# Transposing the input by products with a diagonal of its inverse norms

## The reference

```
def _rmsnorm(x, g):
    y = xf * lax.rsqrt(jnp.mean(xf * xf, axis=-1, keepdims=True) + RMS_EPS)
    return y * g
h = _rmsnorm(x, g_mix) * (1 + sc1) + sh1
z = h @ w_in
```

## Time and profile before

| what | value |
|---|---|
| median of 3 runs | 2197.09 us |
| time of the profiled execution | 2196.86 us |
| its span, first to last instruction | 2195.1 us |
| VectorE busy | 875.9 us (40%) |
| ScalarE busy | 564.1 us (26%) |
| mean granted clock of TensorE | 0.991 |
| DMA, mean over the span | 289 GB/s |
| products of the transposed x (L877) | 9.6 us busy, 64 of them |

### The profile page before, as it was taken

The page is one execution under the profiler, slowest core; times in us unless marked ns, Lnnn a source line. Parts: engine busy times, 40 slices in busy tenths (PEclk is TensorE's granted clock), DMA queues, the critical chain, the costliest instruction groups (busy, mean ns, idle before and its releaser), DMA issues.

```text
span 2195.1 us, 26368 instructions
## 1 busy us (share of the span) xinstructions
PE 2111.6 (96%) x10319; PEld 1373.5 (63%) x10319; DVE 875.9 (40%) x1246; ACT 564.1 (26%) x998; POOL 4.7 (0%) x8
## 2 busy tenths in 40 slices
PE   8999999999999999999999899999999989998986
PEld 5687888888887776888888545353534444444432
DVE  4672667666676665436333301212020302021114
ACT  4253432222246664113222511010101110011102
POOL 0000000000000000000000000000000000000000
PEclk9999999999999999999999999999999999999999
DMA  9947675887860001533522799999999999999998
GB/s 365 388 156 284 243 249 190 322 309 279 282 239 26 25 1 43 188 134 121 171 87 87 299 393 405 426 427 427 427 427 427 429 426 428 426 428 426 427 422 310
DMA packets 144065, 634.83 MB, mean 289 GB/s; under 512 B 11987, under 2 KB 29545, under 8 KB 112757
## 3 DMA queue, kind: packets, MB, share of 16 engines
q1 hardware_dynamic: 139348, 625.38, 72.7%
q10 hardware_dynamic: 4640, 8.40, 1.0%
HBM read 621.15 MB, written 12.58 MB: 289 GB/s over the span
## 4 chain that ended last, share of the span: by engine, by line
PE 84%; DMA 12%; DVE 2%; ACT 0%; issue 0%; SPq 0%; DVEq 0%
PE bank L801 24%; PE bank L1308 23%; PE bank L803 14%; DMA e_wide<-in_w_e_up 10%; PE bank L1280 5%; PE bank L987 5%; PE bank L861 3%; PE bank L1080 3%; PE bank L1300 1%; PE bank L1068 1%; DMA e_slot<-in_w_e_down 1%; PE bank L1301 1%; PE bank L770 1%; PE bank L1290 1%; PE bank L1192 1%; PE bank L828 0%
## 5 line engine op out<-in xcount | busy, mean ns | idle before, releaser
L1308 PE MATMUL bank<-e_wide,xgT 128*64 128x512 f32 x1456 | 404.5, 606 | 42.7 <-DMA e_wide<-in_w_e_up 26.4
L1489 ACT ACTIVATE w_hi<-stage 128x1024 fp32r<-128x1024 f32 (+1 forms) x168 | 175.4, 1044 | 601.7 <-PE bank L801 339.8
L1915 DVE TENSOR_TENSOR w_lo<-stage,w_hi 128x1024 fp32r<-128x1024 f32 (+1 forms) x168 | 202.4, 1205 | 304.2 <-ACT w_hi L1489 303.6
L1308 PEld LDWEIGHTS bank<-e_wide,xgT 128*64 128x64 f32 x1456 | 131.4, 139 | 284.6 <-issue 283.7
L1308 PE MATMUL bank<-e_slot,xgT 128*64 128x512 f32 x584 | 207.0, 598 | 0.0
L1308 PE MATMUL bank<-e_wide,heT 128*64 128x512 f32 x672 | 167.4, 594 | 0.0
L801 PE MATMUL bank<-hT_hi,w_hi 128*128 128x512 f32 x512 | 159.1, 392 | 0.0
L801 PE MATMUL bank<-hT_lo,w_hi 128*128 128x512 f32 x512 | 157.9, 390 | 0.0
L801 PE MATMUL bank<-hT_hi,w_lo 128*128 128x512 f32 x512 | 157.7, 389 | 0.0
L2486 DVE TENSOR_TENSOR x<-x,bank 128x512 f32<-128x512 f32 x128 | 79.6, 683 | 191.9 <-PE bank L1301 190.3
L1990 DVE SCALAR_TENSOR_TENSOR ada_acc<-ada_tile,siluc,ada_acc 128x1024 f32<-128x1024 f32 x116 | 148.7, 1282 | 7.6 <-DMA ada_tile<-in_w_ada 2.0
(11 more groups left out here) (363 smaller groups left out, 2962.1 us busy)
## 6 DMA issues: line engine op xcount, KB each, us to landing
e_wide<-in_w_e_up SPq DMA_DIRECT2D x49, 2048.0 KB, 17.3
e_wide<-in_w_e_gate SPq DMA_DIRECT2D x42, 2048.0 KB, 14.9
e_wide<-in_w_e_down SPq DMA_DIRECT2D x42, 2048.0 KB, 17.2
ada_tile<-in_w_ada SPq DMA_DIRECT2D x156, 512.0 KB, 5.9
stage<-in_w_in SPq DMA_DIRECT2D x96, 512.0 KB, 6.7
e_slot<-in_w_e_gate SPq DMA_DIRECT2D x43, 1024.0 KB, 15.8
e_slot<-in_w_e_down SPq DMA_DIRECT2D x41, 1024.0 KB, 17.0
e_slot<-in_w_e_up SPq DMA_DIRECT2D x30, 1024.0 KB, 10.5
```

Source lines behind the costliest of these rows:

```text
L1308: last = mm(acc[h][64 * e:64 * e + 64, :], stationary(e), weights(h, e), start=first, stop=end)
L1489: A(w_hi[:, c % NSPLIT, :, 0:width], stage[:, c % NSTAGE, :, 0:width], ACT.Copy).then_inc(hi_ready, 1)
L1915: V.tensor_tensor(w_lo[:, c % NSPLIT, :, 0:width], stage[:, c % NSTAGE, :, 0:width], w_hi[:, c % NSPLIT, :, 0:width].bitcast(F32), ALU.sub ...
```

## The change

The tile of x is no longer multiplied by its inverse norms. VectorE writes a diagonal of 128x128 instead, the identity times the inverse norm of each token, and TensorE multiplies each piece of the raw tile by this diagonal with an ordinary float32 product, which gives the transposed and normalised piece at once. The diagonals of the four tiles have a place of their own (`norm_diag`, behind `junk`). The sharing of the copies changes: VectorE copies all four banks of tiles 0 and 1, and in tiles 2 and 3 ScalarE copies two banks and VectorE two. `columns` moves behind the last tile's copies in VectorE's list. The counts of the waits are adapted.

```
+X_ACT = (0, 0, 2, 2)
+        norm_diag = at("A", 40 * KB, "norm_diag", [P, T, P])
@@ TensorE
-                        if i == 0:
-                            pe.wait_ge(xT_act, t)
+                        if i < X_ACT[t - 1]:
+                            pe.wait_ge(xT_act, sum(X_ACT[:t - 1]) + i + 1)
                         else:
-                            pe.wait_ge(xT_dve, 3 * (t - 1) + i)
+                            pe.wait_ge(xT_dve, 4 * (t - 1) - sum(X_ACT[:t]) + i + 1)
-                        last = nc.tensor.transpose(bank[i][:, kk * P:(kk + 1) * P], x_sb[:, t, k * P:(k + 1) * P], ident[:, :])
+                        last = mm(bank[i][:, kk * P:(kk + 1) * P], x_sb[:, t, k * P:(k + 1) * P], norm_diag[:, t, :], start=True, stop=True)
@@ ScalarE
-                for i in range(1 if t < T - 1 else 2):
+                for i in range(X_ACT[t]):
-                    act.wait_ge(xT_act, T + 1)
-                    act.wait_ge(xT_dve, 3 * T - 1)
+                    act.wait_ge(xT_act, sum(X_ACT))
+                    act.wait_ge(xT_dve, 4 * T - sum(X_ACT))
@@ VectorE
-                for i in range(1 if t < T - 1 else 2, 4):
+                for i in range(X_ACT[t], 4):
-                V.tensor_scalar(x_sb[:, t, :], x_sb[:, t, :], rstd[:, 4 + t:5 + t], None, ALU.mult).then_inc(xn_ready, 1)
+                V.tensor_scalar(norm_diag[:, t, :], ident[:, :], rstd[:, 4 + t:5 + t], None, ALU.mult).then_inc(xn_ready, 1)
                 if t:
                     transposed_x(t - 1)
+            transposed_x(T - 1)
             columns()
-            transposed_x(T - 1)
```

## The result

The changed kernel takes 2204.89 us, the median of 7 runs (2202.63 to 2209.24), against 2197.09 us of the kernel before (7 runs, 2195.82 to 2198.16): a ratio of 1.0038, with a 95% interval of 1.0028 to 1.0048. It is 7.8 us slower, beyond the range of the prediction and clear of the 0.2% that can be told. The profiled execution is the longest of the seven, 2209.24 us with a span of 2207.4; a second set of runs of the same kernel gave 2203.96 us (6 runs, ratio 1.0032, interval 1.0020 to 1.0044). All times here are of fast runs: two runs in the slow state, one of e7 with 9814 us and one of the kernel before with 3596 us, are left out.

A forecast was written before the change was run, and what follows sets the result against it. Bound up to 99.5 us by the later of TensorE's work and the saturated load queue; 3.2 us lost by the queue less 1.5 given back is 1.7, taken as 1.6: 2196.86 + 1.6 = 2198.5 us, range 2196.2 to 2202.3.

The forecast's parts named there:

- Bound and place: Up to 99.5 us the later of TensorE's work and the saturated queue's bytes counts; behind it a shift goes through.
- The diagonal: Start of the prologue: writing 128 columns takes 0.17 us instead of 1.29, so TensorE's first piece starts at 9.1, 1.12 gained.
- Two passes for one: TensorE's prologue: 128 instructions instead of 64, at 0.112 us each after a slow 3.55 us for 16; 6.8 us added.
- upper bound of 10.3: TensorE's prologue: most us the products could add, if the slow stretch lasts for all 32 of the first tile.
- Copies and `columns`: Prologue's end: one copy after the last bank, `columns` adds 0.66 us, zero products hidden; TensorE's stream 6.1 us later.
- The stock of the queue: SyncE's waits up to about 63 us: loads left in the queue cover most of its later issues.
- thin place of 61 to 62: DMA share of 0.88 in that microsecond, taken to say that the queue was nearly drained then.
- L: Time lost by the queue at SyncE's three waits, making the second `ada_tile` land later: 3.2 us, bounds 0 and 6.1.
- The first wait: SyncE's issue of 29.99 becomes 36.1; older loads last to 37.45, first new bytes come at 37.7, 0.3 us lost.
- Rival B: The queue starves at SyncE's wait for the first shift sum and the shift goes through: about 2203 us, chance 0.14.
- The clock: Behind the `ada_tile` wait: the wait of 2.39 us goes, the clock should stay up, 1.5 us come back.
- L - 1.5: Net delay behind the `ada_tile` wait: queue loss less the time the clock gives back, 3.2 - 1.5 = 1.7 us.

The follow-up runs named there:

- e7: The kernel before with only the new shares of the copies and the small copies moved behind the last one: 2197.76 us, ratio 1.0006.
- e13: The kernel before with only the transpositions of tiles 2 and 3 issued twice, 32 passes more: 2198.78 us, ratio 1.0012.
- e3: The kernel before with each of the 64 transpositions issued twice and nothing else: 2203.13 us, ratio 1.0029.
- e1: The changed kernel with `columns` ahead of the last tile's copies again: 2202.83 us, ratio 1.0026.
- e2: The changed kernel with transpositions of the raw tile in place of the products, normalisation left out: 2196.39 us, ratio 0.9998.
- e5: The changed kernel with loads of weight chunks 4 to 7 and two tables moved ahead of the first wait that empties the queue: 2204.98 us, ratio 1.0037.
- e4: The changed kernel with loads of weight chunks 10 and 11 moved ahead of the load waiting for the first shift sum: 2201.44 us, ratio 1.0019.
- e10: The changed kernel unaltered, run and profiled a second time: 2203.96 us, ratio 1.0032.
- e6: The changed kernel with products by zeros ahead of the awaited `ada_tile` units, adding nothing to bank 7: 2204.14 us, ratio 1.0034.

## Why the prediction was wrong

*Bound and place: right.* Two clocks run up to about 100 us, TensorE's stream and the bytes of one queue, and behind them a shift goes to the end.

*The diagonal: nearly right.* It took 0.29 us, not 0.17. The first piece came at 9.62, not 9.1; 0.37 of that is the first tile of x, whose squares began at 6.71 instead of 6.34 in this execution.

*Two passes for one: right in kind, 1.6 us short in size.* There are 128 records, as forecast. But 32 of them take 3.77 us in the chain, 0.118 each and not 0.112, which is 0.7 us. A product thus adds 0.236 us where a transposition adds 0.119, a factor of 2.0. The Trainium skill ("TensorE: Matmul & The Clock Gate", Terms) gives the transpose mode as 4 times faster for FP32; the runs differ from it, and they decide. And the slow stretch did not keep its 3.55 us: the third bank of tile 0 was full at 15.1, 24 passes in 5.5 us, so some 8 to 9 more passes were slow, about 0.9 us. The last bank was full at 30.39 instead of 28.3. In all the passes added 8.4 us. The upper bound of 10.3 was added up wrongly: the 16 further slow passes are in the 6.8 already, at 0.112 each, so they add 16 x (0.222 - 0.112) = 1.8, and the bound is 8.6. The measured 8.4 lies just under it.

*Copies and `columns`: right.* One copy after the last bank, 0.6 us of small copies, the zero products hidden under the low weights. Shift 8.2 instead of 6.1, all of it from the terms above.

*The stock of the queue: the step that failed.* That "the thin place of 61 to 62 says that the queue was nearly drained then" gave 2.9 us of cover to an issue at 56.91 (61.4 - 56.91 - 1.6) and L = 3.2. Measured L is 8.85. Of the 5.65 us between them 2.1 are the larger shift, 2.9 the cover that was not there, and 0.6 arose between the late issue (8.26) and the landing. In e7, e13, e3 and the change the landing is 1.0, 0.9, 1.0 and 1.1 times the shift, and with SyncE's old order of loads no run has more than 0.8 us of its shift covered (e1; e2 0.6). The thin place was misread. It lies in SyncE's next pause, of 60.04 to 63.64, when the loads issued from 56.91 on are already under way (the first of them lands at 62.1):

```profile
58.87 1.17 SPq L508 DMA_DIRECT2D sh_tile<-in_w_ada  x2
63.64 0.93 SPq L492 DMA_DIRECT2D ada_tile<-in_w_ada  x2
```

So it doesn't tell how long the older loads lasted; the times to landing do (5.2 and 5.5 us before, 3.6 and 5.3 behind an empty queue). Why the share dips at 61 to 62 was not tested.

The first wait was mis-sized in the same way. The prediction let the queue last until its last load landed, 37.45, and lost 0.3 us there; in the change that load lands at 37.7, 10.5 us after its issue, but the engines had little left to move from 35 us on:

```profile
35.00:36.00 1.00, 0.60 (x3) 0.47 (x3) 1.00 (x2) 0.00 (x0) 0.00 (x0) 1.00 0.28 99
36.00:37.00 1.00, 1.00 (x6) 0.77 (x6) 0.16 (x1) 0.00 (x0) 0.00 (x0) 1.00 0.11 40
37.00:38.00 1.00, 1.00 (x11) 0.47 (x13) 0.00 (x0) 0.00 (x0) 0.00 (x0) 1.00 0.01 4
```

That error alone does no harm: e5 shows that an earlier hole only moves, and the prediction's own sum says so too, since its 0.3 + 0.3 + 2.6 is 64.6 - 61.4, in which the first two waits no longer stand. Rival B had the right place and the right mechanism with a chance of 0.14, and its bound of 6.1 for L was only the too small shift.

*The clock: not given back.* TensorE did wait, 3.1 us in all, and the low clock came back and lasted longer. Where it did stay up, the prediction's sum L - 1.5 fits the start of the first dense block to 0.1 us: it is 6.7 us later in e3 (8.2 - 1.5), 1.9 in e13 (3.4 - 1.5), 4.7 in e1 (6.1 - 1.5), 3.9 in e4 (5.4 - 1.5), 0.1 in e7 (1.5 - 1.5), and 1.2 earlier in e2 (0.2 - 1.5). The medians follow it less closely (+6.4, +2.3, +6.1, +4.7, +0.9 and -0.4); why was not tested. In both profiles of the change the clock fell, and the block starts 11.6 and 9.8 us later where L - 1.5 gives 7.4 and 5.4; the medians, +7.8 and +7.1, lie between.

## What to carry to other kernels

A float32 product against a diagonal costs two passes where the transposition costs one; on an engine without holes that is paid in full, and the vector work it saves was free here but for the first tile's 1 us. A saturated queue hides a late engine only by the stock in it at the last wait that gates its issues, and a share of the DMA engines near 1 does not tell how deep the queue is. Compare instead the time from issue to landing of the first loads behind the wait with that of the same loads on an empty queue; the difference is the stock, here 1.6 us for the first and 0.2 for the second. Loads that wait for nothing, put ahead of that last wait, were worth most of their transfer time (e4: the tile lands 2.3 us less late than TensorE's stream is, against 0.3 in e10, for 2.2 us of loads); put ahead of an earlier wait they were worth nothing (e5).

## What the runs showed of the hardware that was not expected

Whether the lower clock follows a short wait can't be told from its length: waits of 2.39 and 0.30 us (before), 2.13 and 1.00, 2.04 and 0.58 (the change) were followed by a granted clock of 0.50, waits of 2.22 and 0.77 (e3), 1.95 and 0.30 (e13) and 1.60 and 0.32 (e1) were not. The slow stretch at the first pieces varied as well: the first 64 products took 8.97 us in e6, 9.39 in the second profile of the change and 10.05 in the first. The instructions of that stretch are slow (longest 582 ns against a median of 275) while the clock column prints 1.00. A landing can come well after the engines have fallen nearly idle: the last load ahead of the first long pause of SyncE (issued at 27.17) lands at 37.7 in the change, with shares of 0.11 and 0.01 in 36 to 38 us. On an empty queue a load of 512 KB took 3.6 us from issue to landing, while in the full one of before two such loads landed 1.3 us apart (62.1 and 63.4).

```profile
L879 PE MATMUL bank<-norm_diag,x_sb x128: 275/275/582, 9.6 to 30.1; 128*128 128x128 f32 x128
```
